# Routing inside the output projection, a dispatch table by one-hot products, and one stage for routing and experts

## The reference

```python
logits = t @ w_router + b_router                  # t: 2048 x 1024
probs = softmax(logits)
pg = probs.reshape(T, 4, 8)
g_sel = argmax(sum(top_k(pg, 2)[0], -1), -1)      # best group
top_p, top_local = top_k(pg[g_sel], 2)            # two experts of it
expert_idx = g_sel[:, None] * 8 + top_local
gates = top_p / sum(top_p)
y = sum over the two: gate * (silu(t @ w_gate[e]) * (t @ w_up[e])) @ w_down[e]
x = layer_norm(ALPHA * x + (1 + g2) * y)
```

## Time and profile before

| | us |
|---|---|
| median of 3 runs (3180.51 to 3185.98) | 3183.74 |
| the profiled execution | 3186.32 |
| its span | 3184.6 |
| PE busy | 2805.2 (88%) |
| DVE busy | 2182.5 (69%) |
| POOL busy | 1551.1 (49%) |
| ACT busy | 1291.1 (41%) |

### The profile page before, as it was taken

One profiled execution on the slowest core, in us unless ns is written; L12 is line 12 of the kernel. 1 busy time (PEld: TensorE's weight loads), 2 busy tenths in 40 slices (PEclk: granted clock), 3 DMA queues, 4 the chain that ended last, 5 costly groups with the idle time before them and its releaser, 6 DMA issues. The chain is left out here.

```text
span 3184.6 us, 41434 instructions
## 1 busy us (share of the span) xinstructions
PE 2805.2 (88%) x14781; PEld 2326.7 (73%) x14781; DVE 2182.5 (69%) x2531; ACT 1291.1 (41%) x1598; POOL 1551.1 (49%) x852
## 2 busy tenths in 40 slices
PE   7599999999999999999569999924999999999920
PEld 2288888888888888888527888813888888888810
DVE  2467777687777787777533333353888888888868
ACT  1233333333434333333221111113777677677632
POOL 0023334333334333334201232226999999999965
PEclk9799999999999999999779999966999999999965
DMA  6753545434454435352262223235988769587666
GB/s 236 297 200 129 185 150 189 153 125 175 159 186 172 162 133 189 146 185 93 83 250 94 104 105 118 87 122 199 349 308 296 282 246 355 212 291 272 246 240 241
DMA packets 253612, 618.05 MB, mean 194 GB/s; under 512 B 15911, under 2 KB 98603, under 8 KB 244779
## 3 DMA queue, kind: packets, MB, share of 16 engines
q1 hardware_dynamic: 226250, 520.89, 45.3%
q10 hardware_dynamic: 14688, 53.48, 4.2%
q0 software_dynamic: 12544, 41.97, 3.8%
HBM read 608.64 MB, written 99.93 MB: 222 GB/s over the span
## 5 line engine op out<-in xcount | busy, mean ns | idle before, releaser
L1502 DVE TENSOR_TENSOR piece_lo<-piece_raw,piece_hi 128x2048 fp32r<-128x2048 f32 x187 | 563.8, 3033 | 120.1 <-ACT piece_hi L1602 120.0
L1602 ACT CAST piece_hi<-piece_raw 128x2048 fp32r<-128x2048 f32 x280 | 526.4, 1910 | 238.0 <-DVE ye L1662 157.3
L1502 POOL TENSOR_TENSOR piece_lo<-piece_raw,piece_hi 128x2048 fp32r<-128x2048 f32 x93 | 570.4, 6134 | 21.7 <-ACT piece_hi L1602 19.6
L564 PE MATMUL pj<-hm,w_hi 128*128 128x512 f32 x2048 | 532.4, 405 | 24.1 <-DMA hm<-hm_parts 22.1
L823 DVE SCALAR_TENSOR_TENSOR cv<-ub,par,cv 128x512 f32<-128x512 f32 x384 | 385.2, 1003 | 207.6 <-ACT cv L711 198.6
L564 PEld LDWEIGHTS pj<-hm,w_hi 128*128 128x128 f32 x2048 | 378.4, 190 | 99.8 <-DMA hm<-hm_parts 23.7
L528 POOL TENSOR_TENSOR xw<-xw,t 128x512 f32<-128x512 f32 x64 | 96.8, 1512 | 473.4 <-DVE t L899 473.4
L579 PE MATMUL pz<-wz_hi,hm 128*128 128x256 f32 x2048 | 294.7, 289 | 0.3
L579 PEld LDWEIGHTS pz<-wz_hi,hm 128*128 128x128 f32 x2048 | 264.4, 191 | 6.1 <-DVE wz_lo L801 3.1
L716 ACT ACTIVATE th<-cv 128x512 f32<-128x512 f32 x128 | 81.0, 633 | 436.2 <-DVE cv L823 436.2
L564 PE MATMUL pj<-hm,w_lo 128*128 128x512 f32 x1024 | 254.8, 391 | 0.0
(11 more groups left out here) (279 smaller groups left out, 5936.6 us busy)
## 6 DMA issues: line engine op xcount, KB each, us to landing
hm<-hm_parts SPq DMA_DIRECT2D x32, 4096.0 KB, 13.4
piece_raw<-in_w_gate SPq DMA_DIRECT2D x94, 1024.0 KB
piece_raw<-in_w_up SPq DMA_DIRECT2D x94, 1024.0 KB
piece_raw<-in_w_down SPq DMA_DIRECT2D x92, 1024.0 KB
decay<-acum_rows SPq DMA_DIRECT2D x32, 1024.0 KB, 4.7
w_raw<-in_w_in SPq DMA_DIRECT2D x48, 512.0 KB, 8.2
expert_out<-ye ACTq DMA_DIRECT2D x46, 512.0 KB
hm_parts<-hl SPq DMA_DIRECT2D x4, 4096.0 KB, 16.1
```

Source lines behind the costliest of these rows:

```text
L564: mm = nc.tensor.matmul(pj[m % 2][:], wp[m][:, kk, :], hm[b][:, hp, kk, :], start=q == 0, stop=q == 3 * KK - 1)
L1502: v.tensor_tensor(lo[q][:], raw[q][:], hi[q][:].bitcast(F32), ALU.subtract).then_inc(lo_done[q], 1)
L1602: nc.scalar.copy(hi[q][:], raw[q][:]).then_inc(hi_done[q], 1)
```

## The change

1. The row vectors make eight products: the two halves of g2 join them, and DVE spreads its 16 low parts over eight. They land in oh1 and oh2, which serve as buffers, and one row of each goes to memory; the experts read g2 back with one broadcast load.
2. In the output projection DVE routes tiles 0 to 12 (`choose(0, 0, 13)`) behind low(15) and ahead of tile(14), and tiles 13 to 15 at the end. PE computes ranks and totals over all tiles by products (`rank`) in the banks of op0: for 13 tiles ahead of turn(15), for the last three at the end. A product with ones adds tile t's one-hots to the positions of all later tiles.
3. The stage of the routing is gone. At the start of the experts DVE makes the slots from positions and totals, with max(tiles, 1) tiles for each expert; tile 0 is then always expert 0's, so its weights are loaded without a table.
4. The scatter, the read back and the transposition are gone. DVE makes for each token and choice a one-hot of its lane (128 wide) and a one-hot of its tile (66 wide) times the token's number plus 1; PE sums 32 products of them into the table. tile_expert and fresh come from a comparison with the partition index and two products with the identity.
5. DVE splits the first pieces after the table, and only then stores the slots. Each engine waits for the table ahead of the loop.

```diff
 row_vectors
-        rows = [k.g1, k.b2, k.a2]
-        NR = 2 * len(rows)
+        rows = [row[:, n * 512:(n + 1) * 512] for row in (k.g1, k.b2, k.a2) for n in range(2)]
+        rows += [k.oh1[:], k.oh2[:]]
+        NR = len(rows)
+            sp.wait_ge(row_out, NR)
+            for n, row in enumerate((k.oh1, k.oh2)):
+                sp.dma_start(k.g2d[:, n * 512:(n + 1) * 512], row[0:1, :]).then_inc(g2_out, 16)
+            sp.wait_ge(g2_out, 32)
 out_projection, PE
+                if isinstance(j, int) and j >= EARLY:
+                    pe.wait_ge(p_ready, 1)
                 for kk in range(KK):
                     mm = nc.tensor.matmul(lgP[:, bass.ds(j * EXPERTS, EXPERTS)], h2t[:, kk, :], wr[:, kk, :],
...
+                if isinstance(i, int) and i == TT:
+                    rank(0, EARLY)
                 if before:
                     turn(i - 1)
...
+            def rank(t0, t1):
+                pe.wait_ge(eq_ready, 1 if t0 == 0 else 2)
+                if t0 == 0:
+                    pe.wait_ge(t_done, 2 * (TT - 1))
+                    nc.tensor.matmul(position[:], k.below[:], eq, start=True, stop=False, skip_group_check=True)
+                else:
+                    nc.tensor.matmul(position[:, t0 * E:], k.below[:], eq[:, t0 * E:], start=False, stop=False,
+                                     skip_group_check=True)
+                for t in range(t0, t1):
+                    part = eq[:, t * E:(t + 1) * E]
+                    if t + 1 < TT:
+                        nc.tensor.matmul(position[:, (t + 1) * E:].rearrange("p (n e) -> p n e", e=E), k.ones[:],
+                                         part.unsqueeze(1).to_broadcast([P, TT - 1 - t, E]), start=False,
+                                         stop=t == TT - 2, skip_group_check=True)
+                    mm = nc.tensor.matmul(total[:, 0:E], k.ones[:], part, start=t == 0, stop=t == TT - 1,
+                                          skip_group_check=True)
+                mm.then_inc(pos_mm, 1)
             loop(pe, step, 1)
+            rank(EARLY, TT)
 out_projection, ACT
+                    if isinstance(j, int) and j == TT - 1:
+                        power(1, TT - EARLY)
                     act.wait_ge(xa_done, j + 1)
...
+                if isinstance(i, int) and i == TT - 2:
+                    power(0, EARLY)
 out_projection, DVE
                 if in_loop(i, 0, TT - 1):
                     low(i + 1, 1 - b)
+                if isinstance(i, int) and i == TT - 2:
+                    choose(0, 0, EARLY)
...
+            choose(1, EARLY, TT - EARLY)
+            dve.wait_ge(pos_mm, 2)
 experts, SP
             load(0, range(GU))
-            sp.wait_ge(scat, 16 * 2 * TT)
-            sp.dma_start(idr[:], k.slotd.rearrange("(a b) c -> a (b c)", b=P)).then_inc(id_in, 16)
+            sp.dma_start(g2[:], k.g2d[0].partition_broadcast(P)).then_inc(g2_in, 16)
+            sp.wait_ge(ids_ready, 1)
             loop(sp, step)
 experts, POOL
-            for i in range(TT):
-                for slots in (k.slot_a, k.slot_b):
-                    nc.gpsimd.indirect_dma_start(
-                        out=k.slotd[:], out_offset=bass.IndirectOffsetOnAxis(ap=slots[:, i:i + 1], axis=0),
-                        in_=k.tok[:, i:i + 1], in_offset=None).then_inc(scat, 16)
-            pool.wait_ge(scat, 16 * 2 * TT)
 experts, PE
-            pe.wait_ge(id_in, 16)
-            nc.tensor.transpose(yp[0][:, 0:NTAB], idr[:], k.ident[0:NTAB, 0:NTAB]).then_inc(id_tr, 1)
+            for c in range(2):
+                pe.wait_ge(marks_done, c + 1)
+                for t in range(TT):
+                    if t % 8 == 0:
+                        pe.wait_ge(lanes_done, 2 * c + t // 8 + 1)
+                    mm = nc.tensor.matmul(yp[0][:, 0:NTAB], lanes[c][t // 8][:, t % 8, :], marks[c][:, t, :],
+                                          start=c == 0 and t == 0, stop=c == 1 and t == TT - 1)
+            mm.then_inc(ids_mm, 1)
+            pe.wait_ge(te_done, 1)
+            for n in range(2):
+                mm = nc.tensor.matmul(yp[1][0:1, n * P:(n + 1) * P], te[:, n:n + 1], k.ident[:], start=True, stop=True)
+            mm.then_inc(te_mm, 1)
 experts, DVE
-            for q in range(3):
-                low_part(dve, nc.vector, q, 0)
-            dve.wait_ge(id_tr, 1)
-            nc.vector.tensor_copy(k.ids[:], yp[0][:, 0:NTAB]).then_inc(ids_ready, 1)
+            link(v.tensor_scalar(nt_i[:], total[:, 0:E], float(P - 1), None, ALU.add))
+            link(v.tensor_scalar(nt_i[:], nt_i[:], 7, None, ALU.arith_shift_right))
+            link(v.tensor_scalar(nt[:], nt_i[:], 1.0, None, ALU.max))
...
+            for c in range(2):
+                own = slice(c * TT, (c + 1) * TT)
+                link(v.tensor_tensor(marks[c], along(k.tidx[:, 0:NTAB], TT, NTAB), over(tf[:, own], TT, NTAB),
+                                     ALU.is_equal))
+                v.tensor_tensor(marks[c], marks[c], over(tok1[:], TT, NTAB), ALU.mult).then_inc(marks_done, 1)
+                for n in range(2):
+                    half = pf[:, c * TT + 8 * n:c * TT + 8 * n + 8]
+                    v.tensor_tensor(lanes[c][n], along(k.tidx[:], 8, P), over(half, 8, P), ALU.is_equal
+                                    ).then_inc(lanes_done, 1)
...
+            dve.wait_ge(ids_mm, 1)
+            v.tensor_scalar(k.ids[:], yp[0][:, 0:NTAB], -1.0, 0.0, ALU.add, ALU.max).then_inc(ids_ready, 1)
+            dve.wait_ge(te_mm, 1)
+            link(v.tensor_copy(k.tile_expert[0:1, :], yp[1][0:1, 0:NTAB]))
+            v.tensor_copy(k.fresh[0:1, :], yp[1][0:1, P:P + NTAB]).then_inc(table_ready, 1)
+            low_part(dve, nc.vector, 0, 0)
+            low_part(dve, nc.vector, 1, 0)
             xt_low(0)
+            low_part(dve, nc.vector, 2, 0)
+            for c, slots in enumerate((k.slot_a, k.slot_b)):
+                link(v.tensor_copy(slots[:], sl_i[:, c * TT:(c + 1) * TT]))
+            dve.wait_ge(g2_in, 16)
             last = loop(dve, step)
```

More of the change, by code:

```diff
@@ L43 @@
 NTAB = MAXT + 2
+EARLY = 13
 YTILES = DI // P
@@ L1056, in _, with out_projection @@
             dve.wait_ge(chain, 5)
-def out_projection(nc, k, w_hi, w_lo, lgP):
+def out_projection(nc, k, w_hi, w_lo, lgP, first):
     with ExitStack() as ctx:
@@ L1071, in out_projection @@
         rstd = sb("rstd", [P, 1])
-        op = [[ps(f"op{b}{n}", [P, 512]) for n in range(2)] for b in range(2)]
-        tp = [ps(f"tp{n}", [P, 512]) for n in range(2)]
+        E, NE = EXPERTS, TT * EXPERTS
+        rb = sb("rb", [P, E])
+        mx, sm = sb("mx", [P, TT]), sb("sm", [P, TT])
+        m1, m2, i1 = (sb(n, [P, EARLY * EGROUPS]) for n in "m1 m2 i1".split())
+        op = [first, [ps(f"op1{n}", [P, 512]) for n in range(2)]]
+        tp = [ps(f"tp{n}", [P, 512]) for n in range(2)]
+        cand = ps("cand", [P, 512])
+        position, total = first
+        flat = yraw[:].rearrange("p m t -> p (m t)")
+        eq = flat[:, 0:NE]
+        gs, gh = (flat[:, 2 * EARLY * E + n * EARLY * EGROUPS:2 * EARLY * E + (n + 1) * EARLY * EGROUPS] for n in range(2))
+        rb_in, p_ready, exp_done, eq_ready, pos_mm, chain = (sem(n) for n in (
+            "rb_in p_ready exp_q eq_ready pos_mm chain_q").split())
         (y_in, wr_in, hi_done, lo_done, o_mm, t_done, r_done, bn_done, mv_done, ve_done, rstd_done, nmr_done,
@@ L1359, in first_max @@
                 link(v.tensor_tensor(hot, values, over(m, n, w), ALU.is_equal))
[L1361 to L1364 removed]
+                c = rows(cand[:, 0:n * w], w)
@@ L1404, in _ @@
-            link(v.tensor_tensor(rows(cand, E), rows(cand, E), along(base[:], TT, E), ALU.add))
-            for oh, slots in ((oh1, k.slot_a), (oh2, k.slot_b)):
-                link(v.tensor_tensor(pm[:], cand[:], oh[:], ALU.mult))
-                link(v.tensor_reduce(slf[:], rows(pm, E), AX.X, ALU.add))
-                link(v.tensor_copy(slots[:], slf[:]))
-            link(v.tensor_tensor(cmp[:], along(end[:], NTAB, E), over(k.tidx[:], NTAB, E), ALU.is_le))
-            link(v.tensor_reduce(ef[:], cmp[:], AX.X, ALU.add))
@@ L1429, in experts @@
+            low(0, 0)
+            loop(dve, step, 1)
+            choose(1, EARLY, TT - EARLY)
+            dve.wait_ge(pos_mm, 2)
+def experts(nc, k, first):
     with ExitStack() as ctx:
@@ L1442, in experts @@
         ye = [sb(f"ye{b}", [P, D]) for b in range(2)]
-        xp = [ps(f"xp{n}", [P, 512]) for n in range(2)]
+        g2 = sb("g2", [P, D])
+        E = EXPERTS
+        nt_i, lp_i = sb("nt_i", [P, E], I32), sb("lp_i", [1, 1], I32)
+        nt, end, base, cmp = (sb(n, [P, E]) for n in "nt end base cmp".split())
+        slf, pf, tf = (sb(n, [P, 2 * TT]) for n in "slf pf tf".split())
+        sl_i, p_i, t_i = (sb(n, [P, 2 * TT], I32) for n in "sl_i p_i t_i".split())
+        tok1, before = sb("tok1", [P, TT]), sb("before", [P, 1])
+        te = sb("te", [P, 2])
+        cand, pm = th[:], a[:]
```

(29 more changed lines are left out.)

228 lines of the change are left out of this document (100 added, 128 removed).

## The result

| | us |
|---|---|
| before, median of 5 runs (3178.14 to 3187.74) | 3183.74 |
| after, median of 5 runs (3165.22 to 3167.23) | 3166.3 |
| ratio, with its 95% interval | 0.9946 [0.9932, 0.9961] |
| the profiled execution, before and after | 3186.32 and 3165.22 |
| its span, before and after | 3184.6 and 3163.5 |

The change makes the kernel faster, by 17.4 us in the medians and 21.1 us in the profiled executions. The forecast was 34.4. The sign is right and the time lies inside the range, near its dear end; about half of the gain is missing, and the sum of the prediction is what has to be explained.

A forecast was written before the change was run, and what follows sets the result against it. A serial chain between output projection and experts, 127 us with PE mostly idle, was taken as the bound. First product 50.4 us earlier, less 16.0 for row vectors, gives -34.4: 3183.7 to 3149.3 us, range 3133 to 3169.

The forecast's parts named there:

- rival A: Start of the experts: the weight stream sets the pace, 6 us less gain, 3155 us; 22 in 100.
- rival C: Expert loop: more tiles, 50 in place of 46 from three empty experts on, +73 us, 3222; 3 in 100.
- rival B: Output projection: the early routing is hidden and the 15.8 us stall gone, 3133.5 us; 8 in 100.
- a second step of more than 17 us: Experts: a second step starting more than 17 us behind the first would show the forecast wrong.
- Parts 2 and 3: Output projection: routing 13 tiles early stalls PE 15.8 us; routing the last three takes 9.9 us, experts start at 2112.9.
- the early part does not pay by itself: Routing: 15.8 + 9.9 us for what took 18.9; the gain comes from elsewhere.
- Part 1: Row vectors: the two added rows of g2 make the stage 16 us longer, bounds +8 to +22.
- in proportion that is 18.4 us a pair: Row vectors: a pair moves 6.3 MB instead of 7.0, so takes 18.4 us instead of 20.4.
- The bound of +22 us: Row vectors: the dear bound, if each pair of row products still takes 20.4 us.
- Part 4: Start of the experts: table by products, ids ready at 2133.2 against 2181.98, first product at 2144.2 instead of 2194.65.
- A clock that rises after the first quarter: Table products on PE: end at 2132.9, between 2131.4 with a fast clock and 2137.7 with none.
- 11 us (10 to 13): Start of the experts: time from ids to the first product, 12.7 us before, with DMA engines free for the gather.

The follow-up runs named there:

- the run with halves: The changed kernel with each w_ada block of the row products loaded and freed in two halves; 3145.75 us, ratio to before 0.9873.
- the run with ten products ahead: The changed kernel with ten products that nobody reads put on PE in front of the table products; 3157.47 us, ratio to before 0.9917.

## Why the prediction was right, and where it was wrong

Events are taken as their distance from before, in us; the prediction's numbers are its own.

| event | forecast | measured |
|---|---|---|
| last row product read | +15.6 | +20.8 |
| low(15) done | +16 | +20.5 |
| first product of the experts | -34.4 | -22.1 |
| span | -34.4 | -21.1 |

From low(15) on, in steps:

| from | to | forecast | measured |
|---|---|---|---|
| low(15) | experts start | 70.3 | 68.5 |
| experts start | ids written | 20.3 | 23.9 |
| ids written | first product | 11 | 17.0 |

**The frame held.** The serial part between the output projection and the experts was the right place to look. What was cut from it came out at the end; the experts kept 46 tiles at 18.3 us, with a second step of 19.5 us where before had 19.6, so neither the weight stream (rival A) nor more tiles (rival C) came true, and the early routing was not hidden (rival B). One sign was badly set: a second step of more than 17 us was to show the forecast wrong, but the second step of before, and the 18.3 us of every later one, are longer than that, so the sign says nothing.

**Parts 2 and 3 held.** The choice of 13 tiles took 16.9 us (forecast 17.1), PE's wait 11.1 (11.8), the stall in all 14.4 (15.8, although the prediction's terms 13.1 + 1.0 + 1.5 give 15.6, and its 2083.4 goes by that), the ranking 10.1 (10.1). The sentence that the early part does not pay by itself was too strong: the run without it is 4.7 us slower, because the ranking then stands in the open, 14.2 us of it. The prediction compared only DVE's times, and left the ranking that the early part hides out of that comparison.

**Part 1 failed in its term, "in proportion that is 18.4 us a pair".** The pairs took 19.5, 19.5 and 20.3; that is 4.2 us over three pairs. The DMA share of 0.97 in the second pair was read as a limit of bytes. The first pair of before was as long, 20.6 us, at a share of 0.82 and 302 GB/s, the pairs of after were nearly so with less to carry, and the run with halves shows 16 us for the same bytes. The pair was one product and one load in turn, and taking out 0.7 MB did not shorten the load: it was 10.4 us in the second pair of before and is 10.7 now. What the first two pairs did lose is 1.1 us of their first product (10.0 to 8.9), where the granted clock is 0.91 and 0.88 over the pair instead of 0.83. Another 1.1 us is the later start of the first product. The bound of +22 us held it all. The prediction also passed over what the move of g2 gives up: in before its products stood beside the routing on DVE, where they held PE's ranking up by at most 2.5 us (eq is written at 2108.02, the product into pre starts at 2110.56). In the row vectors the same two rows cost 19.5 us. Another place for them, such as PE's idle time at the start of the experts, was not tried.

**Part 4 failed in two terms.** "A clock that rises after the first quarter" was a choice between the bounds 2131.4 and 2137.7, and the dear bound was the true one: the clock rose in no quarter, and from the start of the experts to ids it took 3.6 us more. The run with ten products ahead shows that the low clock is the cause: it gets 5.0 us back. The other term is "11 us (10 to 13)" from ids to the first product, taken because "the gather has the DMA engines for itself". It did not have them. The issue on POOL stretched from 1.01 to 5.23 us beside DVE's piece_lo, the loads were issued before it ended, and from its end to PE's read it took 7.0 us, as in before. So the term missed twice, by 4.2 us of issue and by the 1.7 us that the free engines were to give, together nearly all of the 6.0. (Its starting row was misread too: from ids to xp it was 9.3 us in before, 2181.98 to 2191.28; 8 us is the way from the gather's issue.) The prediction expected DVE's piece_lo to meet POOL's own piece_lo and asked only how POOL slows DVE; it met the gather's issue, and the price was the other way round, 7.8 us by the run with DVE's pieces ahead of ids. It lay outside the term's bounds; the whole stayed in its range only because the other bounds were wide. The trace of before already had a sign of it. There a scatter's issue takes 0.96 us, but the three that were issued beside a piece_lo of DVE take 2.17 to 2.87, this one beside the piece_lo at 2141.91:

```profile
2142.16 2.87 POOL L1525 DMA_INDIRECT token_by_slot<-tok,slot_b  x1 [0.30 <-issue]
```

The rule that it named (the Trainium skill, Advanced Engine Details and Errata, Miscellaneous Facts: GpSimd and VectorE share an interface, and VectorE's instructions with two SBUF inputs conflict) is borne out by this trace, only for the instruction that the prediction did not price.

The sum of the misses from the first row product to the first expert product is 4.5 - 1.8 + 3.6 + 6.0 = 12.3 us, which is 34.4 - 22.1. The last microsecond is lost behind it.

## What to carry to other kernels

A wait for a DMA beside a high DMA share does not prove that bytes set the pace: look at the rate in small steps, and if it falls to zero once in each round, cut the buffer's hand-over finer before counting bytes. Work moved off the end of a stage is free only behind the last thing that its engine owes to the busy one; here one tile later made the same routing free. Where a short GpSimd instruction such as a gather's issue stands on the critical chain, keep wide VectorE operations away from it, and look whether a late issue falls behind loads that it was to precede. For products that follow a pause of PE, let the sum's dear bound have the low clock for their whole length: the 64 of the table never left it here, while the ranking in the run with all tiles at the end did after 5.7 us. And before moving work to a stage that sets the time, ask what it cost where it was.

## What the runs showed of the hardware that was not expected

- POOL's issue of a gather took 1.22 us with DVE idle, 2.34 beside 1.24 us copies with one input, and 4.82 to 5.24 (five traces) beside two 2.24 us subtractions of two SBUF tiles; a second gather that began inside such a subtraction took 2.33. From the start of the issue to the landing it was 12.2 us for the first gather of the changed kernel and 4.4 with DVE idle. More is lost than the 4.0 us of the issue, since the weight loads were issued before the long one ended.
- 64 float32 products of 66 columns, 13.9 us without a gap, ran at 0.50 to the end. The ranking of the run with all tiles at the end also began at 0.50, with products of 512 and 480 columns, and was at the high level from 2131.2 on, 5.7 us later. Why the one rose and the other did not was not tried further.
- The two DMA queues together held 392 to 396 GB/s at a share of 1.04 over 46 us, where whole blocks gave 305 to 323 on average.
